# A two-layer transformer kernel: the cross attention's unit order, one unit's score buffer, and the order of two weight loads

## The reference, cut to what matters

```python
x = x + y @ w_out[l]
x = x + memory_cross_attention(rmsnorm_2(x, norm_cross[l]), mem_n, w_q_x[l], w_kv_x[l], w_o_x[l])
x = x + swiglu(rmsnorm_2(x, norm_ffn[l]), w_gu[l], w_down[l])

def memory_cross_attention(hn, mem_n, w_q, w_kv, w_o):      # hn: 256 x 1024, 4 heads of 64
    q = (hn @ w_q).reshape(b, s, H_X, HEAD_DIM)
    kv = (mem_n @ w_kv).reshape(b, m, 2, H_X, HEAD_DIM)
    sc = jnp.einsum('bqhd,bmhd->bhqm', q, kv[:, :, 0]).astype(jnp.float32) * HEAD_DIM ** -0.5
    p = jax.nn.softmax(sc, axis=-1).astype(hn.dtype)
    o = jnp.einsum('bhqm,bmhd->bqhd', p, kv[:, :, 1]).reshape(b, s, H_X * HEAD_DIM)
    return o @ w_o
```

## Time and profile before

| | |
|---|---|
| median of 3 runs | 1628.68 us (1627.95 to 1630.46) |
| the profiled execution's own time | 1628.68 us |
| its span in the trace | 1626.7 us |
| TensorE busy | 1566.8 us, 96% |
| VectorE busy | 880.8 us, 54% |
| ScalarE busy | 647.8 us, 40% |
| chain that ended last | PE 80%, DMA 10%, DVE 8%, ACT 1% |

### The profile page before, as it was taken

The page is one execution under the profiler, slowest core; times in us unless marked ns, Lnnn a source line. Parts: engine busy times, 40 slices in busy tenths (PEclk is TensorE's granted clock), DMA queues, the critical chain, the costliest instruction groups (busy, mean ns, idle before and its releaser), DMA issues.

```text
span 1626.7 us, 25754 instructions
## 1 busy us (share of the span) xinstructions
PE 1566.8 (96%) x10979; PEld 1265.0 (78%) x10979; DVE 880.8 (54%) x1300; ACT 647.8 (40%) x1022; POOL 62.9 (4%) x30
## 2 busy tenths in 40 slices
PE   8988989889899999999999999999999999999998
PEld 7877434434334449989899799999999899799998
DVE  5944211212112139667867576647576878476654
ACT  2034111112111116464664554435364674554443
POOL 0000000000000000024000000000006000000000
PEclk9988999999999999999999999999999999999999
DMA  9165999999999995736333565464553543365550
GB/s 349 47 258 207 402 427 429 427 430 427 430 427 428 427 406 201 236 114 208 130 139 121 161 202 185 178 243 176 185 184 127 174 156 130 108 201 184 181 205 29
DMA packets 126915, 393.81 MB, mean 242 GB/s; under 512 B 4321, under 2 KB 60001, under 8 KB 114017
## 3 DMA queue, kind: packets, MB, share of 16 engines
q1 hardware_dynamic: 126816, 392.38, 63.7%
HBM read 386.34 MB, written 1.05 MB: 238 GB/s over the span
## 4 chain that ended last, share of the span: by engine, by line
PE 80%; DMA 10%; DVE 8%; ACT 1%; issue 1%; SPq 0%; DVEq 0%; ACTq 0%
PE psum L1270 11%; PE psum L996 11%; PE psum L997 11%; PE psum L1004 11%; DMA ring<-w 8%; PE psum L1335 4%; DVE outs L2008 3%; PE psum L1622 2%; PE psum L1621 2%; PE psum L1619 2%; PE psum L1481 2%; PE psum L1233 2%; PE psum L1428 1%; PE psum L1429 1%; PE psum L1427 1%; PE psum L956 1%
## 5 line engine op out<-in xcount | busy, mean ns | idle before, releaser
L996 PE MATMUL psum<-h_parts,w_hi 128*128 128x256 f32 x1472 | 364.6, 286 | 0.2 <-DVE w_lo L641 0.2
L997 PE MATMUL psum<-h_parts,w_lo 128*128 128x256 f32 x1472 | 355.1, 279 | 0.0
L641 DVE TENSOR_TENSOR w_lo<-raw_a,w_hi 128x1024 fp32r<-128x1024 f32 x184 | 222.4, 1222 | 121.4 <-ACT w_hi L1641 120.5
L996 PEld LDWEIGHTS psum<-h_parts,w_hi 128*128 128x128 f32 x1472 | 276.3, 188 | 12.4 <-issue 9.3
L997 PEld LDWEIGHTS psum<-h_parts,w_lo 128*128 128x128 f32 x1472 | 277.4, 188 | 0.2
L1641 ACT ACTIVATE w_hi<-raw_a 128x1024 fp32r<-128x1024 f32 x202 | 210.9, 1055 | 162.2 <-PE psum L1004 64.9
L1004 PE MATMUL psum<-h_parts,w_hi 128*128 128x256 f32 x1472 | 201.9, 279 | 0.0
L1270 PE MATMUL psum<-ring,outs 128*64 128x512 f32 x720 | 167.5, 622 | 26.8 <-DMA ring<-w 25.6
L1004 PEld LDWEIGHTS psum<-h_parts,w_hi 128*128 128x128 f32 x1472 | 184.7, 188 | 0.0
L1270 PEld LDWEIGHTS psum<-ring,outs 128*64 128x64 f32 x720 | 58.1, 143 | 133.5 <-issue 133.5
L641 DVE TENSOR_TENSOR w_lo<-raw_b,w_hi 128x1024 fp32r<-128x1024 f32 x92 | 111.4, 1222 | 51.7 <-ACT w_hi L1641 51.3
(11 more groups left out here) (311 smaller groups left out, 2533.4 us busy)
## 6 DMA issues: line engine op xcount, KB each, us to landing
ring<-w SPq DMA_DIRECT2D x76, 2048.0 KB, 16.4
raw_a<-w_in SPq DMA_DIRECT2D x20, 2048.0 KB, 8.1
raw_a<-w_gu SPq DMA_DIRECT2D x32, 1024.0 KB, 7.8
raw_b<-w_in SPq DMA_DIRECT2D x10, 2048.0 KB, 8.4
wp<-w SPq DMA_DIRECT2D x8, 2048.0 KB, 18.5
hs<-w SPq DMA_DIRECT2D x8, 2048.0 KB, 22.9
raw_b<-w_gu SPq DMA_DIRECT2D x12, 1024.0 KB, 7.3
raw_a<-w_down SPq DMA_DIRECT2D x8, 1536.0 KB, 6.5
```

Source lines behind the costliest of these rows:

```text
L641: return eng.tensor_tensor(chunk_part(w_lo, n), chunk_raw(n), chunk_part(w_hi, n).bitcast(F32), ALU.subtract)
L996: mm(to, hi[:, k, :], h_hi[:, k, :], start=(k == 0), stop=False)
L997: mm(to, lo[:, k, :], h_hi[:, k, :], start=False, stop=False)
```

## The change

- The load of the query weights comes ahead of the memory's (`q_x` is piece 21 and `kv_x` piece 22).
- Unit 27's scores no longer have a duo of their own. They go into the first bank of the duo `xkv`, where the keys were before they were copied out, one head into each half of it; the second head waits until unit 24's turn is done, and the first goes ahead in a step of its own (`scores_half`).
- The order of steps: scores 25 stands ahead of the second query chunk, scores 26 ahead of probs 25, all four turns ahead of all `apply` steps, and both parts of `cross_v` later. ScalarE copies a turn of unit 26 or 27 only after the output of unit 24 or 25 (the buffer of turned probabilities is shared).
- The values' copy is announced on `xheads_ready`, and no longer frees the duo.
- In `cross_o` the first four products of the first half need only unit 25's output; the rest waits for unit 27's.
- ScalarE has a square root of one number behind the copy of the keys, which loads the table of the square root there.

```diff
-                + [("up", b) for b in (0, 2, 1)] + [("out", 0), ("out", 1), ("kv_x",), ("q_x",), ("o_x",)]
+                + [("up", b) for b in (0, 2, 1)] + [("out", 0), ("out", 1), ("q_x",), ("kv_x",), ("o_x",)]
...
-        + [("out", 19, 0), ("out", 20, 1), ("norm", "cross"), ("cross_k", 21), ("cross_q", 22, 0),
-           ("sums", "cross"), ("scores", 24), ("exp", 24), ("cross_q", 22, 1), ("scores", 25), ("exp", 25), ("probs", 24),
-           ("cross_v", 21, 0), ("probs", 25), ("turn", 24), ("scores", 26), ("exp", 26), ("cross_v", 21, 1), ("probs", 26),
-           ("turn", 25), ("scores", 27), ("apply", 24), ("exp", 27), ("turn", 26), ("apply", 25), ("probs", 27), ("turn", 27),
-           ("apply", 26), ("apply", 27), ("cross_o", 23), ("norm", "ffn")]
+        + [("out", 19, 0), ("out", 20, 1), ("norm", "cross"), ("cross_k", 22), ("cross_q", 21, 0),
+           ("sums", "cross"), ("scores", 24), ("exp", 24), ("scores", 25), ("cross_q", 21, 1), ("exp", 25), ("probs", 24),
+           ("scores", 26), ("exp", 26), ("probs", 25), ("scores_half", 27), ("turn", 24), ("cross_v", 22, 0),
+           ("probs", 26), ("scores", 27), ("exp", 27), ("turn", 25), ("probs", 27), ("cross_v", 22, 1), ("turn", 26), ("turn", 27), ("apply", 24),
+           ("apply", 25), ("apply", 26), ("apply", 27), ("cross_o", 23), ("norm", "ffn")]
...
-        held = w[0] in ("index_weights", "gates_head", "up_head", "gates", "probs", "scores", "turn", "apply", "cross_q", "square_b", "sums", "evac", "rope", "index_product", "subln_sums", "outs_high", "outs_low", "subln", "subln_factors") or w[0] == "exp"
+        held = w[0] in ("scores_half", "index_weights", "gates_head", "up_head", "gates", "probs", "scores", "turn", "apply", "cross_q", "square_b", "sums", "evac", "rope", "index_product", "subln_sums", "outs_high", "outs_low", "subln", "subln_factors") or w[0] == "exp" or w == ("cross_v", 22, 0)
...
+    seats["u_27"] = seats["xkv"]
...
+        def scores_of(u):
+
+            return view(duo(f"u_{u}"), 0, 2, SEQ if u == 27 else 512)
...
+                        elif w == ("scores", 27):
+                            pe.wait_ge(probsT_done, l * N_UNITS + 25)
                         enter(pe, f"u_{u}", l)
-                        for r in range(2):
+                        for r in ((0,) if kind == "scores_half" else (1,) if u == 27 else range(2)):
...
                         if u == 24:
-                            freed(pe, "xkv", l)
+                            pe.wait_ge(xheads_ready, l * 3 + 3)
...
+                        enter(pe, "xo_0", l)
+                        freed(pe, "u_25", l)
+                        out_products(0, range(4), (0,))
                         freed(pe, "u_27", l)
...
                         act_e.wait_ge(probsT_done, l * N_UNITS + u + 1)
+                        if u >= 26:
+                            act_e.wait_ge(attn_done, l * N_UNITS + u - 1)
...
                         copy(kx, view(duo("xkv"), 0, 2, SEQ)).then_inc(xheads_ready, 1)
+                        f(rtok[:, 12:13], eps[:], ACT.Sqrt)
...
-                        copy(vx, view(duo("xkv"), 512, TT, SEQ)).then_inc(free_of("xkv"), 1)
+                        copy(vx, view(duo("xkv"), 512, TT, SEQ)).then_inc(xheads_ready, 1)
```

More of the change, by code:

```diff
@@ L301, in tenants @@
         elif kind == "scores":
-            names.append(f"u_{w[1]}")
+            names += [f"u_{w[1]}"] if w[1] != 27 else []
         elif kind == "subln_sums":
@@ L322 @@
 DUO_OF = {"p_vb": 3, "p_idx": 2, "i_0": 2, "i_1": 0, "p_qc": 3, "p_kc": 1, "p_vc": 0, "subln": 0, "up_0_0": 3, "up_0_1": 1, "up_2_0": 2, "up_2_1": 3, "up_1_0": 0, "up_1_1": 1,
-          "out_0": 0, "out_1": 1, "u_24": 1, "u_25": 2, "u_26": 0, "u_27": 3}
+          "out_0": 0, "out_1": 1, "u_24": 1, "u_25": 2, "u_26": 0}
 def seat(names, before, at):
@@ L1464, in _ @@
                         chunk_head(i, o, duo(name)[:, o * SEQ:(o + 1) * SEQ], l, range(GATE_HEAD))
-                    elif kind == "scores":
+                    elif kind in ("scores_half", "scores"):
                         u = w[1]
@@ L1474, in _ @@
                         elif u == 24:
-                            pe.wait_ge(xheads_ready, l * 2 + 2)
+                            pe.wait_ge(xheads_ready, l * 3 + 2)
                         elif u == 26:
                             freed(pe, "xq", l)
+                        elif w == ("scores", 27):
+                            pe.wait_ge(probsT_done, l * N_UNITS + 25)
                         enter(pe, f"u_{u}", l)
-                        for r in range(2):
+                        for r in ((0,) if kind == "scores_half" else (1,) if u == 27 else range(2)):
                             rows = slice(64 * r, 64 * r + 64)
-                            last = mm(duo(f"u_{u}")[:, r * 512:r * 512 + nk], qb[rows, cc, qt * P:(qt + 1) * P],
+                            last = mm(scores_of(u)[:, r, 0:nk], qb[rows, cc, qt * P:(qt + 1) * P],
                                       kb[rows, cc, 0:nk], start=True, stop=True)
-                        last.then_inc(scores_done, 1)
+                        if kind == "scores":
+                            last.then_inc(scores_done, 1)
                     elif kind == "turn":
@@ L1584, in _, with out_products @@
                         raw_arrived(pe, i, l)
-                        freed(pe, "u_27", l)
[L1586 to L1596, removed]
+                        wo = view(raw_of(i), 0, 2, D)
+                        def out_products(half, os, ks):
+                            to = view(duo(f"xo_{half}"), 0, 4, SEQ)
+                            for o in os:
+                                oo = half * 4 + o
+                                for k in ks:
+                                    last = mm(to[:, o, :], wo[:, k, oo * P:(oo + 1) * P], ox[:, k, :],
+                                              start=(k == 0 and o % 2 == 0), stop=(k == 1), skip_group_check=True)
+                            return last
+                        enter(pe, "xo_0", l)
+                        freed(pe, "u_25", l)
+                        out_products(0, range(4), (0,))
+                        freed(pe, "u_27", l)
+                        for bank in range(2):
+                            out_products(0, (2 * bank, 2 * bank + 1), (1,)).then_inc(xo_bank, 1)
+                        enter(pe, "xo_1", l)
+                        for bank in range(2):
+                            out_products(1, (2 * bank, 2 * bank + 1), (0, 1)).then_inc(xo_bank, 1)
                         pe.wait_ge(xo_bank, l * 4 + 4)
@@ L2368, in _ @@
                             v.wait_ge(probsT_done, l * N_UNITS + u - 2)
-                        s, d = probs[:, u % 3, :, 0:nk], view(duo(f"u_{u}"), 0, 2, 512)[:, :, 0:nk]
+                        s, d = probs[:, u % 3, :, 0:nk], scores_of(u)[:, :, 0:nk]
                         if ukind == "X":
```

## The result

The changed kernel takes 1635.32 us (median of 8 runs, 1633.53 to 1637.36), the kernel before 1628.6 us in the same measurement (1624.75 to 1631.69). The ratio is 1.0039, 95% interval 1.0028 to 1.0049: slower by 6.7 us. The forecast was 1633.8 us, range 1629.0 to 1638.0, with 0.71 on slower by over 0.2%.

What follows compares the result with a forecast made beforehand. TensorE, busy 96% of the span, was taken as the bound. Two layers at 3.07 us make 6.1, less 3.0 for the second layer's clock, plus 2.0 for one new slow stretch: 1628.68 + 5.1 = 1633.8 us, range 1629.0 to 1638.0.

Steps and rivals of the forecast that it cites:

- The chunk at the head of the queues: Cross attention's front: chunk 85 waits for its load ahead of norm and additions, making the sums 4.87 us later a layer.
- The tail: Cross attention's end: three old waits of 2.53 us go, new ones return 1.1; gain taken as 1.5 us a layer.
- The additions ahead of the feed-forward: VectorE before the feed-forward's first product: additions no longer wait for chunks 85 to 87; 0.3 us gained a layer.
- The clock: Second layer's 3.0 us slow stretch goes; a new one behind the thinned front, likeliest once, costs 2.0 us.
- The case with two: Rival: a new slow clock stretch in both layers, 1635.8 us; chance 0.2.
- The lull at unit 27: TensorE's 1.85 us wait ahead of unit 27's turn: goes, so the second layer no longer pays 3.0 us there.
- The early table load: Square root's table load behind the keys' copy: 1.28 us off sums to scale factor, costed at nothing since TensorE has cover.
- The rival in which the load counts in full: Softmax chain paces the middle, table load gains 2 x 1.28 us: 1631.2; chance 0.13 together with an earlier landing.
- The rival on the faster side: Piece 24's load lands early enough, some 3.3 us after issue, so the front is hardly delayed: 1622.7 us; chance 0.07.

Runs made afterwards that it cites:

- the kernel with the moved chunk: The changed kernel with chunk 85's split and low part held back until after the cross norm's squares; 1621.9 us, ratio 0.9964 to the kernel before.
- the swap alone: The kernel before with only the loads of query weights and memory weights traded; 1643.93 us, ratio 1.0104 to the kernel before.

## Why the prediction was right, and what was mis-sized

- **The chunk at the head of the queues.** Right, and read from the order of instructions beside the trace. I had 4.87 us; it was 5.36 and 4.55, mean 4.96. The landing was the uncertain part. From the issue at 884.36 to the split at 893.25 it is 8.89 us in the first layer, and 1397.68 - 1389.61 = 8.07 in the second, where I took 8.25, the upper bound that the rows gave. So one layer lay above that bound, and the 0.82 between the two landings is the 0.81 between the two fronts.
- **The tail.** I had a gain of 1.5 us; at full clock it is 1.59 (30.53 to 28.94). That the size fits is partly luck. The three new waits are 0.56, 0.72 and 0.29, together 1.57, where I had 0.5, 0.45 and 0.15, so of the 2.53 us of old waits only 0.96 are gained. The other 0.6 is a term that I had put at nothing: between sums and output product, waits left out, TensorE's work takes 17.65 us in the new order (19.22 - 1.57) and took 18.29 in the old one (20.82 - 2.53). The largest part is the four applications, which stand together now: 2.2 us (from start to start 1.12 and 1.08, waits left out) instead of 2.7.
- **The additions ahead of the feed-forward.** I had 0.3 us for taking the load out of this path. It was nothing, and its mechanism was wrong: the feed-forward starts 7.48 us behind the start of the output product in the kernel with the moved chunk, 7.45 in the first layer before. A 0.30 us gap stands there whoever is named as its end.
- **The clock.** I had one slow stretch at 2.0 us as the likeliest; there were two at 1.5 each. The case with two was a rival at 1635.8, and it is the one that came. The lull at unit 27 went as forecast, and its slow stretch with it. The new sum is 2 x (4.96 - 1.59 + 1.51) - 3.0 = 6.8 us, which is what the two stretches show. The 3.0 belongs to one traced execution, though; with the early load alone the same slow stretch cost 1.4, so that this sum meets the 6.7 us between the medians so closely is partly luck.
- **The early table load.** "I cost it at nothing" was right only as a difference to the kernel before. The working behind it, that scores and query chunk cover the way to the root and that without the cover it would be a gain, failed: in the new order unit 25's scores wait until the root has been taken out of the sums' duo, and the early load shortens that way. Without it each layer is 1.2 us longer. The rival in which the load counts in full had its 1.28 us as a gain on the softmax chain; here they are a loss avoided, on TensorE's own path.
- **The rival on the faster side** was the right mechanism with the wrong condition: 1622.7 was worked out for a load that lands in time, and 1621.9 came when the chunk was moved behind the norm instead.

Why the clock falls behind one lull and not behind another of the same size stays open. The wait of 1.85 us at unit 27 stands in both layers of three traces (before, the swap alone, the early load alone): the first layer of the kernel before and of the one with the early load alone came through it at 1.00, and in the other four layers the output product took 8.42 to 9.68 us instead of 7.14.

## What to carry to other kernels

When two loads trade places, look at what the freed slot lets start early, and where its first consumer then stands: a prefetch that is nobody's hurry can head an in-order queue in front of urgent work, on every engine that takes part in it. Such an edit may have one good and one bad effect, and one condition in the scheduler keeps the good one; do each part alone before the whole is judged. Moving an instruction ahead of its cover brings its waits, on memory areas too, onto the path, so an edit beside it that seems idle may be what pays for the move.

## What the runs showed of the hardware that was not expected

Four products that nobody reads, put into a wait of 1.94 us, kept the granted clock at 1.00 in both layers, where without them it fell to 0.50 (0.81 to 0.85 over windows of 5 us), and saved 1.5 us a layer. Two equal waits of 1.85 us in the kernel before had a clock of 1.00 behind one and 0.50 behind the other. Where it fell behind such a wait, the output product took 8.42, 9.10, 9.60 and 9.68 us in four layers, for 7.14 at full clock.
